# Two RMS norms in a row: the second from three running means, and the residual add folded into it

## What is computed

```python
x = x + gate1 * rms_norm(y_x, norm_g[l, 1])
hx = rms_norm(x, norm_g[l, 2]) * (1.0 + sc2) + sh2
x = x + gate2 * rms_norm(swiglu(hx, w_ffn_in[l], w_ffn_out[l]), norm_g[l, 3])
# the next layer begins with
hx = rms_norm(x, norm_g[l, 0]) * (1.0 + sc1) + sh1
```

## Time and profile before

| what | value |
|---|---|
| median of three runs | 3379.0 us (3375.65 to 3379.71) |
| the profiled execution's own time | 3387.04 us |
| its span in the profile | 3385.2 us |
| PE busy | 3125.1 us, 92% of the span |
| DVE busy | 1502.8 us, 44% |
| ACT busy | 1164.2 us, 34% |
| POOL busy | 829.0 us, 24% |

### The profile page before, as it was taken

One profiled execution on the slowest core, in us unless ns is written; L12 is line 12 of the kernel. 1 busy time (PEld: TensorE's weight loads), 2 busy tenths in 40 slices (PEclk: granted clock), 3 DMA queues, 4 the chain that ended last, 5 costly groups with the idle time before them and its releaser, 6 DMA issues.

```text
span 3385.2 us, 79208 instructions
## 1 busy us (share of the span) xinstructions
PE 3125.1 (92%) x34382; PEld 2501.4 (74%) x34382; DVE 1502.8 (44%) x2358; ACT 1164.2 (34%) x2403; POOL 829.0 (24%) x518
## 2 busy tenths in 40 slices
PE   7998898999999998999999888989899989889998
PEld 5777677777777786888888666767677767768886
DVE  4455464644354652200044464756564446330033
ACT  4433333423333434211112353433343345342222
POOL 2211111111223222122223221111111333434453
PEclk9999999999999999999999989999999999999999
DMA  5424243334454352111111233423233343522222
GB/s 210 134 97 136 84 125 119 117 124 141 129 179 159 133 179 69 41 65 62 62 50 62 81 95 102 125 64 121 64 120 107 99 131 114 183 67 98 99 87 75
DMA packets 246714, 364.56 MB, mean 108 GB/s; under 512 B 154080, under 2 KB 155376, under 8 KB 245904
## 3 DMA queue, kind: packets, MB, share of 16 engines
q1 hardware_dynamic: 226976, 294.57, 27.4%
q10 hardware_dynamic: 14976, 35.66, 2.7%
q0 software_dynamic: 4464, 29.92, 2.5%
HBM read 290.88 MB, written 69.21 MB: 106 GB/s over the span
## 4 chain that ended last, share of the span: by engine, by line
PE 77%; DVE 6%; ACT 4%; issue 4%; DMA 2%; DVEq 2%; POOLq 1%; PEld 1%; SPq 1%; POOL 0%; PEldq 0%; ACTq 0%
PE banks L281 20%; PE banks L282 18%; PE banks L283 18%; PE banks L1675 2%; PE banks L1023 2%; PE banks L1686 1%; PE banks L1639 1%; PE banks L395 1%; PE banks L1678 1%; PE banks L1051 1%; PE banks L2048 1%; PE banks L1736 1%; POOLq L2419 1%; DVE arena L597 1%; PE banks L2059 1%
## 5 line engine op out<-in xcount | busy, mean ns | idle before, releaser
L283 PE MATMUL banks<-hx_rounded,slot_rounded 128*128 128x512 f32 (+1 forms) x1624 | 577.4, 356 | 0.0
L906 POOL TENSOR_TENSOR slot_rounded<-slot,branch_weights_high 128x512 fp32r<-128x512 f32 x188 | 246.5, 1333 | 1286.5 <-ACT branch_weights_high L901 1285.2
L281 PE MATMUL banks<-hx_high,weight_parts 128*128 128x512 f32 (+1 forms) x1512 | 538.1, 356 | 10.9 <-DVE hx_low L545 10.4
L281 PE MATMUL banks<-hx_rounded,branch_weights_high 128*128 128x512 f32 (+1 forms) x1280 | 498.9, 390 | 43.8 <-DVE arena L1364 8.7
L282 PE MATMUL banks<-hx_low,weight_parts 128*128 128x512 f32 (+1 forms) x1512 | 538.3, 356 | 0.0
L283 PE MATMUL banks<-hx_high,weight_parts 128*128 128x512 f32 (+1 forms) x1512 | 536.3, 355 | 0.0
L282 PE MATMUL banks<-resid_rounded,branch_weights_high 128*128 128x512 f32 (+1 forms) x1280 | 454.2, 355 | 0.0
L283 PEld LDWEIGHTS banks<-hx_rounded,slot_rounded 128*128 128x128 f32 x1624 | 313.7, 193 | 44.6
L281 PEld LDWEIGHTS banks<-hx_rounded,branch_weights_high 128*128 128x128 f32 x1280 | 246.9, 193 | 123.7 <-issue 74.0
L281 PEld LDWEIGHTS banks<-hx_high,weight_parts 128*128 128x128 f32 x1512 | 286.8, 190 | 55.4 <-issue 14.3
L283 PEld LDWEIGHTS banks<-hx_high,weight_parts 128*128 128x128 f32 x1512 | 286.5, 189 | 41.0
(11 more groups left out here) (263 smaller groups left out, 5870.0 us busy)
## 6 DMA issues: line engine op xcount, KB each, us to landing
slot<-in_w_mix SPq DMA_DIRECT2D x120, 512.0 KB, 4.1
slot<-in_w_ffn_in SPq DMA_DIRECT2D x88, 512.0 KB, 3.3
arena<-chunk_inputs SPq DMA_DIRECT2D x48, 640.0 KB, 4.5
arena<-in_w_ada SPq DMA_DIRECT2D x50, 512.0 KB, 5.2
slot<-in_w_ffn_out SPq DMA_DIRECT2D x44, 512.0 KB, 3.3
slot<-in_w_ada SPq DMA_DIRECT2D x40, 512.0 KB, 4.3
chunk_inputs<-arena SPq DMA_DIRECT2D x80, 256.0 KB, 3.8
arena<-side_projections POOLq DMA_DIRECT2D x16, 1152.0 KB, 6.3
```

Of the source, the lines that this page charges most:

```text
L281: first = nc.tensor.matmul(out, w_hi, x_hi, start=start, stop=False)
L283: return first, nc.tensor.matmul(out, w_lo, x_hi, start=False, stop=stop)
L906: last = nc.gpsimd.tensor_tensor(slots_r[g % 3][:, half], slots[g % 3][:, half], weights_high(g)[:, half], ALU.subtract)
```

## The change

- The second norm's mean is no longer taken from the finished sum. With r the first norm's factor, the mean of (x + r y)^2 is mean(xx) + 2 r mean(xy) + r^2 mean(yy). DVE, POOL and PE gather the three means while the update's tiles are produced; DVE combines them (`add_and_norm_dve`), ACT takes Ln and Exp (`mean_square_act`). The squares and means of the new residual (`stats_act`, and `stats_pe` for these uses) go.
- In the out projection of both layers DVE makes yy and xy (`y_part`, `x_part`), POOL makes xx (`square_residual`).
- In the second half of layer 0's down projection DVE's slab loop gets nine more tensor_tensor instructions per two slabs and four memsets ahead of it; four sums of squares become one matmul pair; for the last four tiles DVE and POOL make the products behind the loop (`products_dve`, `squares_of_updates`).
- The residual adds run inside the norm, tile by tile: even tiles on DVE, odd ones on POOL (`add_pool`, which stands behind `first_rests` on POOL's queue, or behind `lora_pool` at the second boundary). The store of the residual tiles (SP) waits for them in the same order as before.

```diff
+        def add_tile(e, half, k, lo, Y):
+            nc_e = nc.gpsimd if k % 2 else nc.vector
+            nc_e.tensor_tensor(NSQ[k % 2][:, lo:T], Y[:, k, lo:T], NRS[:, lo:T], ALU.mult)
+            e.drain()
+            nc_e.tensor_tensor(RES[:, k, lo:T], RES[:, k, lo:T], NSQ[k % 2][:, lo:T], ALU.add).then_inc(pool_added.sem if k % 2 else added.sem, 1 if k % 2 else 2)
+            e.drain()
+        def add_pool(pool, l, half, segs, Y):
+            pool.wait_ge(rs_made, 4 * l + 2 * half + 2)
+            pool.wait_ge(sq_made.sem, sq_made.ready(use_of_sum(l, half), KD - 1))
+            for k in range(1, KD, 2):
+                add_tile(pool, half, k, SEGS[segs[0]][0], Y)
+        def add_and_norm_dve(dve, l, half, segs, norm_segs, Y, pairs):
+            lo = SEGS[segs[0]][0]
+            out = SUM_RS[half]
+            dve.wait_ge(rs_made, 4 * l + 2 * half + 2)
+            use = use_of_sum(l, half)
+            dve.wait_ge(sq_used.sem, sq_used.ready(use, KD // 4 - 1))
+            for s in segs:
+                c0, c1 = SEGS[s]
+                nc.vector.tensor_tensor(out[:, c0:c1], pair(pairs[1])[s], NRS[:, c0:c1], ALU.mult)
+            dve.drain()
+            dve.wait_ge(sq_used.sem, sq_used.ready(use, KD // 2 - 1))
+            for s in segs:
+                c0, c1 = SEGS[s]
+                nc.vector.scalar_tensor_tensor(out=out[:, c0:c1], in0=pair(pairs[0])[s], scalar=2.0, in1=out[:, c0:c1], op0=ALU.mult, op1=ALU.add)
+            dve.drain()
+            nc.vector.tensor_tensor(out[:, lo:T], out[:, lo:T], NRS[:, lo:T], ALU.mult)
+            dve.drain()
+            dve.wait_ge(sq_used.sem, sq_used.ready(use, KD - 1))
+            for s in segs:
+                c0, c1 = SEGS[s]
+                nc.vector.tensor_tensor(out[:, c0:c1], pair(pairs[2])[s], out[:, c0:c1], ALU.add)
+            dve.drain()
+            nc.vector.tensor_scalar(out[:, lo:T], out[:, lo:T], 0.0, 1.0, ALU.max, ALU.mult).then_inc(ap_scaled.sem, 1)
+            add_tile(dve, half, 0, lo, Y)
+            if half == 0:
+                dve.sem_inc(f_mid.sem, 2)
+            def before(k):
+                if k % 2:
+                    dve.wait_ge(pool_added.sem, pool_added.ready(2 * l + half, k // 2))
+            def following(k):
+                if k % 2 == 1 and k + 1 < KD:
+                    add_tile(dve, half, k + 1, lo, Y)
+            norm_dve(dve, 2 * l + half + 1, 1 - half, norm_segs, out, before, following)
+        def mean_square_act(act, l, half, segs):
+            lo = SEGS[segs[0]][0]
+            act.wait_ge(ap_scaled.sem, ap_scaled.ready(2 * l + half + 1, 0))
+            nc.scalar.activation(SUM_RS[half][:, lo:T], SUM_RS[half][:, lo:T], ACT.Ln, bias=one[:, 0:1])
+            act.drain()
+            nc.scalar.activation(SUM_RS[half][:, lo:T], SUM_RS[half][:, lo:T], ACT.Exp, scale=-0.5).then_inc(rs_made, 1)
...
+        X_AFTER = {3: (0, 1), 4: (2, 3), 5: (4, 5), 6: (6,)}
         def out_dve(dve, l):
             use, lo = 4 * l + 1, SEGS[segs_of(l)[0]][0]
-            for m in range(1, KD - 1):
+            xy_t, yy_t = [x[:, lo:T] for x in OUT_TERMS]
+            xy, yy = [x[:, lo:T] for x in OUT_SUMS[0:2]]
+            def y_part(m):
+                nc.vector.tensor_tensor(yy if m == 0 else yy_t, Y[:, m, lo:T], Y[:, m, lo:T], ALU.mult)
+                dve.drain()
+                if m:
+                    nc.vector.tensor_tensor(yy, yy, yy_t, ALU.add)
+                    dve.drain()
+            def x_part(k):
+                nc.vector.tensor_tensor(xy if k == 0 else xy_t, RES[:, k, lo:T], Y[:, k, lo:T], ALU.mult)
+                dve.drain()
+                if k:
+                    nc.vector.tensor_tensor(xy, xy, xy_t, ALU.add)
+                    dve.drain()
+            for m in range(KD - 1):
                 dve.wait_ge(sq_made.sem, sq_made.ready(use, m))
-                last = nc.vector.tensor_tensor(SQ_SUM[:, lo:T], NSQ[0][:, lo:T] if m == 1 else SQ_SUM[:, lo:T], NSQ[m % 2][:, lo:T], ALU.add)
-                last.then_inc(sq_used.sem, 2 if m == 1 else 1)
-                dve.drain()
+                if m:
+                    last = nc.vector.tensor_tensor(SQ_SUM[:, lo:T], NSQ[0][:, lo:T] if m == 1 else SQ_SUM[:, lo:T], NSQ[m % 2][:, lo:T], ALU.add)
+                    last.then_inc(sq_used.sem, 2 if m == 1 else 1)
+                    dve.drain()
+                y_part(m)
+                if m == 3:
+                    dve.wait_ge(resid_back, 16 * (l + 1))
+                for k in X_AFTER.get(m, ()):
+                    x_part(k)
             dve.drain().then_inc(sq_summed.sem, 1)
+            dve.wait_ge(sq_made.sem, sq_made.ready(use, KD - 1))
+            nc.vector.tensor_tensor(yy_t, Y[:, KD - 1, lo:T], Y[:, KD - 1, lo:T], ALU.mult)
+            nc.vector.tensor_tensor(xy_t, RES[:, KD - 1, lo:T], Y[:, KD - 1, lo:T], ALU.mult)
+            dve.drain().then_inc(sq_made.sem, KD)
+        OUT_PAIRS = (4, 0, 2)
+        FFN_PAIRS = (2, 4, 6)
-            for source, made in ((SQ_SUM, sq_summed), (NSQ[(KD - 1) % 2], sq_made)):
-                pe.wait_ge(made.sem, made.ready(use if made is sq_made else l, KD - 1 if made is sq_made else 0))
-                for s in segs:
-                    last = nc.tensor.matmul(stats_bank(use)[s], MEAN_D, source[:, SEGS[s][0]:SEGS[s][1]], start=made is sq_summed, stop=made is sq_made)
-            last.then_inc(sq_used.sem, 1)
+            xy, yy, xx = OUT_SUMS
+            xy_last, yy_last = OUT_TERMS
+            xy_pair, yy_pair, xx_pair = OUT_PAIRS
+            pe.wait_ge(sq_summed.sem, sq_summed.ready(l, 0))
+            means_pe(l, 0, segs, SQ_SUM, 6, True, False)
+            means_pe(l, 0, segs, yy, yy_pair, True, False)
+            means_pe(l, 0, segs, xy, xy_pair, True, False)
+            pe.wait_ge(sq_made.sem, sq_made.ready(use, KD - 1))
+            means_pe(l, 0, segs, NSQ[(KD - 1) % 2], 6, False, True).then_inc(sq_used.sem, 1)
+            pe.wait_ge(sq_made.sem, sq_made.ready(use + 1, KD - 1))
+            means_pe(l, 0, segs, yy_last, yy_pair, False, True).then_inc(sq_used.sem, KD // 4)
+            means_pe(l, 0, segs, xy_last, xy_pair, False, True).then_inc(sq_used.sem, KD // 4)
+            pe.wait_ge(pool_squares.sem, pool_squares.ready(l, 0))
+            means_pe(l, 0, segs, xx, xx_pair, True, True).then_inc(sq_used.sem, KD // 2)
...
+        def square_residual(pool, l, k):
+            lo = SEGS[segs_of(l)[0]][0]
+            total, part = OUT_SUMS[2][:, lo:T], OUT_XX[:, lo:T]
+            if k == 0:
+                pool.wait_ge(resid_back, 16 * (l + 1))
+            nc.gpsimd.tensor_tensor(part if k else total, RES[:, k, lo:T], RES[:, k, lo:T], ALU.mult)
+            pool.drain()
+            if k:
+                last = nc.gpsimd.tensor_tensor(total, total, part, ALU.add)
+                if k == KD - 1:
+                    last.then_inc(pool_squares.sem, 1)
+                pool.drain()
         def out_pool(pool, l):
             for m in range(KD):
                 pool.wait_ge(y_high.sem, y_high.ready(l, 0, m + 1))
@@ -2538,6 +2666,10 @@
                 pool.drain().then_inc(slab_used[m % 4], 1)
                 if m == 0:
                     pool.dma_start(resid[:, :], a["resid_dram"] if l else a["x"]).then_inc(resid_back, 16)
+                if m >= 3:
+                    square_residual(pool, l, m - 3)
+            for k in range(KD - 3, KD):
+                square_residual(pool, l, k)
...
+            if l == DEPTH - 1:
+                for h in range(2):
+                    each_out_slab(dve, h, slab, begun=h == 0)
+            else:
+                each_out_slab(dve, 0, slab, begun=True)
+                slab(1, 0, 0, 0)
...
+                dve.wait_ge(sq_made.sem, sq_made.ready(4 * l + 3, 3))
+                for x in (xy, yy, xx, squares):
+                    nc.vector.memset(x, 0.0)
+                with dve.Fori(0, NJ // 4 - 1) as i:
+                    slab(1, i * 2 + 1, 1, i)
+                    x_low, x_high, y, sq = [x[:, bass.ds(i + at, 1), lo:T].rearrange("p a t -> p (a t)") for x, at in ((RES, 0), (RES, 4), (YF, 0), (SQUARE_TILES, 0))]
+                    nc.vector.tensor_tensor(term[0], x_low, y, ALU.mult)
+                    nc.vector.tensor_tensor(term[1], y, y, ALU.mult)
+                    dve.drain()
+                    nc.vector.tensor_tensor(xy, xy, term[0], ALU.add)
+                    nc.vector.tensor_tensor(yy, yy, term[1], ALU.add)
+                    nc.vector.tensor_tensor(squares, squares, sq, ALU.add)
+                    dve.drain()
+                    slab(1, i * 2 + 2, 2, i)
+                    nc.vector.tensor_tensor(term[0], x_low, x_low, ALU.mult)
+                    nc.vector.tensor_tensor(term[1], x_high, x_high, ALU.mult)
+                    dve.drain()
+                    nc.vector.tensor_tensor(xx, xx, term[0], ALU.add)
+                    dve.drain()
+                    nc.vector.tensor_tensor(xx, xx, term[1], ALU.add)
+                    dve.drain()
```

(82 more changed lines are left out.)

28 lines of the change are left out of this document (21 added, 7 removed).

## The result

The changed kernel takes 3437.3 us (median of four runs, 3434.87 to 3438.59) against 3379.4 for the kernel before beside it (3375.65 to 3381.07). The ratio is 1.0173, 95% interval 1.016 to 1.0185: **slower by 58 us**. The prediction said 3438. The profiled execution has a span of 3436.7 us where before had 3385.2.

A forecast was written before the change was run, and what follows sets the result against it. PE bounds the kernel, with 77% of the chain, so norm changes count only at three boundaries where it stands still. Terms 30 + 4 + 25 = 59 on 3387.0 gave 3446, adjusted by 8 to 3438 us; own range 3415 to 3460, with the DVE-first case 3397 to 3460.

The forecast's parts named there:

- The step on which all hung: Shared port: two-input DVE and POOL instructions alternate, one waiting for the other; a handover saves about 0.14 us.
- the one without sharing: Rival: these forms do not share; first boundary -7, third -1, second -8, total 3363 us; chance 0.11.
- the one in which DVE goes ahead: Rival: DVE goes first each time, POOL gets gaps; +13, third +12, second +2, total 3406; chance 0.2.
- Whole durations: Rival: no handover saving, 0.14 more for some 45 instructions per boundary, +6 at two, 3450; chance 0.08.
- priced at 1.84 alone for want of a row: POOL's 768-column price, taken between 1.29 and 2.39; a multiply by itself was given the subtract's price.
- +30: First boundary: cost from sums ready at 1348.8 and the norm sharing the port; PE's first FFN products end at 1420.
- the prediction's 8.9: First boundary: PE's four means, three slow at about 2.6 and the rest warm at 1.43, from 1348.8 to about 1357.7.
- 17 and 13: First boundary's split of +30: the late sum some 17, the shared norm the rest.
- +25: Third boundary: cost with 512 columns; sums at 3000.1, norm start about 3016, rest of tile 3 at 3031.5 against 3005.85.
- +4: Second boundary: sum of loop +6 to +7, norm start -9 and longer norm +6.5.
- not 1.7: Down projection loop: DVE and POOL need 18.5 per two slabs against 16.8, 1.7 over, four times; +6 to +7.
- my chain: Second boundary: products, three means, DVE's chain, Ln and Exp; norm start 24.5 behind PE's last product against 33.2, -9.

## Why the prediction was right, and where it was not

**The port.** The step on which all hung is shown. Two-input DVE work stood at 2.06 to 3.16 us beside POOL and at 0.96 alone (512 columns: 1.35 to 2.76 and 0.69); from 1292.0 to the sums it was 55.7 us where 56.8 was predicted, and moving POOL's squares to DVE moved the end by 0.2. Both rivals in which DVE is not held up, the one without sharing and the one in which DVE goes ahead, would have shown 0.96 beside POOL's work; they are out. Whole durations would have put the sums 6 later than predicted, and they came 1 earlier. The closeness is in part luck: POOL's multiply of a tile by itself, priced at 1.84 alone for want of a row, takes 1.47, which makes the port's sum 2 us too high, and DVE's six instructions without a partner, priced as if they had one, make it 1 too low. With 1.47 the whole durations come to 60.4, still 4.7 over what was measured. One row of the prediction is misread: L2740 did not stand inside a POOL rest, it overlapped the last 0.42 of one and the start of the next. That such passes are not held up is shown by the last section.

The Trainium skill (SBUF — State Buffer, Who interferes with whom) has this as an exclusive lock. The trace agrees with it in the waiting (2.94 for 0.96), but not to the full length: a DVE instruction and a rest in turn take 3.01, where their own durations make 3.35.

**First boundary: +27.0 for +30.** Sums at 1347.7 (predicted 1348.8), Ln at 1355.8 (1357.7), last rest of tile 3 ended at 1389.5 (1391.5). Each was 1 to 2 us under its term. The four means took 7.98 for 8.9: two of them, and not three, ran at half clock (2.6 each), the others took 1.29. (By its own prices the prediction's 8.9 should have read 9.2.) But how I split the cost was off. By the runs the sums are 25.6, giving POOL the odd adds costs 6.0 (61.8 against 55.7 without sums; 4.5 with them), and the form with three means gives back 4.6: net 21.0 and 6.0, where I had 17 and 13.

**Third boundary: +21.7 for +25.** Sums 22.1 us behind the copy of the last tile (23.0 predicted), norm start 37.3 (38.9), last rest of tile 3 ended 51.0 (54.4). The adds inside the norm cost 5.6 there, where I had 2.8 and 4.6, together 7.4.

**Second boundary: +12.7 for +4.** This is the term of the sum that was mis-sized: it cost three times what was forecast, and it missed in three places. The loop is 2.33 over per two slabs (19.13 against 16.8), not 1.7: the sum of DVE's own durations was right, but 0.27 to 0.56 of issue in each slab was left out. The norm start comes 3.9 earlier and not 9, for my chain had DVE's passes there at their free durations:

```profile
1940.23 2.60 DVE L2928 TENSOR_TENSOR arena<-resid,hx 128x768 f32<-128x768 f32 x1 [7.83 <-ACT arena L489]
...
1965.04 1.96 DVE L650 TENSOR_TENSOR arena<-arena 128x768 f32<-128x768 f32 x1
...
1968.99 2.56 DVE L623 TENSOR_TENSOR arena<-hx,arena 128x768 f32<-128x768 f32 x1
1971.62 2.40 DVE L625 TENSOR_TENSOR resid<-resid,arena 128x768 f32<-128x768 f32 x1
```

POOL's adds start at 1958.51, 6.5 us ahead of L650, and DVE's three passes alternate with them (1.96, 2.56 and 2.40 for 0.96 each): 4.0 of the 5 missed. I had counted that sharing at the first boundary and left it out here; with all adds on DVE the norm starts 5.4 earlier. From its start to its last tile the norm is 8.1 longer, where I had 6.5.

Two misses of -3 and one of +9 nearly cancel, 61.8 by stages for 59, and the medians lie another 4 below the stages, 57.9. So the agreement of 3437 with 3438 is luck in part; the steps agree to 3 us at two boundaries and miss by 9 at the second.

**The gain at which the form aims** is small even with free sums: 12 us at the norm's start, 3 to 5 where PE uses the tiles. Not tried: making the squares on ACT, whose norm tiles (L572, 1.30 for two) kept their length beside both engines.

## What to carry to other kernels

Add up the time of all two-input SBUF work of DVE and POOL in the stretch before asking which engine has room: both were under half busy on the page (44% and 24%), and in the stretch their sum was what bounded. Work that feeds a wait has to be costed with everything that is queued on the other engine of the pair, its next stage's work too. An engine that stands for PE a few us per slab can take a few instructions for nothing (three sums, 5.9 us won), but not nine per two slabs (8.5 us lost).

## What the runs showed of the hardware beyond that

- The two engines took turns strictly: with both queues full, DVE's and POOL's instructions alternated one for one, though DVE's take 0.96 alone and POOL's 1.47 to 2.39.
- DVE's one-input work with SBUF on both sides is held up too: the pair of L555 (tensor_scalar, 256 columns) took 3.79 beside POOL and 0.87 alone, L657 0.91 and 0.56. Passes that read PSUM are not: the pair of L655 took 1.02 from 1362.48 on, wholly inside a POOL multiply that ran from 1361.76 to 1364.07.
- On POOL a multiply of a tile by itself is cheaper than one of two tiles: 1.47 (L2654) against 1.80 (L2657, L623) at 768 columns, 1.04 against 1.26 at 512, with DVE idle. The prediction had put both at 1.84.
